# Gate panels moved in between index scores and attention heads, kept in device memory until the projections

## The reference, cut to what matters

```
(fq, fk, fv, ff, dq, dk, dv, iq, ik, iw, mq, g) = jnp.split(u @ w_in[l], SPLIT_POINTS, axis=-1)
o_a = fox_attention(fq, fk, fv, logf)                       # 8 heads of 64, causal with a forget bias
o_b = dsa_attention(dq, dk, dv, iq, ik, iw, k_sel)          # 8 heads of 64 on the 128 best keys by index score
o_c = memory_attention(mq, km, vm)                          # 4 heads of 128 on 256 memory rows
branches = jnp.stack([o_a, o_b, o_c], axis=2)
proj = jnp.einsum('bsnw,nwd->bsnd', branches, w_branch[l])  # 512 -> 1024 for each branch
gates = jax.nn.sigmoid(g.reshape(B, S, N_BRANCHES, D))
h = h + jnp.sum(gates * proj, axis=2) @ w_out[l]
```

## Time and profile before

| | us |
|---|---|
| runs | 2604.82, 2604.82, 2608.97 (median 2604.82) |
| the profiled execution | 2603.45 |
| its span, first to last instruction | 2601.7 |
| PE busy | 2461.6 (95%) |
| DVE busy | 1348.6 (52%) |
| ACT busy | 875.1 (34%) |
| POOL busy | 120.6 (5%) |
| mean granted clock of PE | 0.959 of full |

### The profile page before, as it was taken

One profiled execution on the slowest core, in us unless ns is written; L12 is line 12 of the kernel. 1 busy time (PEld: TensorE's weight loads), 2 busy tenths in 40 slices (PEclk: granted clock), 3 DMA queues, 4 the chain that ended last, 5 costly groups with the idle time before them and its releaser, 6 DMA issues.

```text
span 2601.7 us, 32023 instructions
## 1 busy us (share of the span) xinstructions
PE 2461.6 (95%) x12976; PEld 1952.7 (75%) x12976; DVE 1348.6 (52%) x2043; ACT 875.1 (34%) x1461; POOL 120.6 (5%) x156
## 2 busy tenths in 40 slices
PE   7999999997989999999999998888898899999997
PEld 6888888874444888888888886777776687788886
DVE  5444344426683546544433673443375663777723
ACT  4222223321455223322222344334346243433321
POOL 0000000000233000000000000132200000000000
PEclk9999999897699999999999997899898999999998
DMA  5333333320000333333333331000031132233331
GB/s 164 97 97 93 102 102 109 90 69 1 1 1 1 96 90 109 98 97 97 97 95 97 92 83 49 2 2 2 2 90 41 49 97 81 73 97 97 99 95 49
DMA packets 366419, 189.04 MB, mean 73 GB/s; under 512 B 11328, under 2 KB 363840, under 8 KB 366272
## 3 DMA queue, kind: packets, MB, share of 16 engines
q1 hardware_dynamic: 366272, 187.00, 25.2%
HBM read 184.87 MB, written 2.10 MB: 72 GB/s over the span
## 4 chain that ended last, share of the span: by engine, by line
PE 88%; DVE 7%; ACT 3%; issue 1%; DMA 0%; POOL 0%; DVEq 0%; SPq 0%; ACTq 0%
PE ps L429 22%; PE ps L431 22%; PE ps L430 22%; PE ps L677 2%; PE ps L948 1%; PE ps L696 1%; PE ps L915 1%; PE ps L1879 1%; PE ps L1881 1%; PE ps L1880 1%; PE ps L811 1%; PE ps L1373 1%; PE ps L1368 1%; PE ps L541 1%; PE ps L1363 1%
## 5 line engine op out<-in xcount | busy, mean ns | idle before, releaser
L429 PE MATMUL ps<-u_hi,w_hi 128*128 128x512 f32 (+1 forms) x1800 | 706.4, 392 | 3.0 <-DVE w_lo L362 2.1
L430 PE MATMUL ps<-u_lo,w_hi 128*128 128x512 f32 (+1 forms) x1800 | 703.9, 391 | 0.0
L431 PE MATMUL ps<-u_hi,w_lo 128*128 128x512 f32 (+1 forms) x1800 | 703.7, 391 | 0.0
L362 DVE TENSOR_TENSOR w_lo<-w_raw,w_hi 128x1024 fp32r<-128x1024 f32 (+2 forms) x366 | 422.6, 1155 | 271.8 <-ACT w_hi L378 270.9
L378 ACT ACTIVATE w_hi<-w_raw 128x1024 fp32r<-128x1024 f32 (+2 forms) x366 | 365.7, 1000 | 445.7 <-PE ps L431 417.1
L429 PEld LDWEIGHTS ps<-u_hi,w_hi 128*128 128x128 f32 (+1 forms) x1800 | 336.0, 187 | 79.7 <-DVE w_lo L362 3.0
L430 PEld LDWEIGHTS ps<-u_lo,w_hi 128*128 128x128 f32 (+1 forms) x1800 | 336.0, 187 | 75.2 <-issue 1.6
L431 PEld LDWEIGHTS ps<-u_hi,w_lo 128*128 128x128 f32 (+1 forms) x1800 | 336.0, 187 | 74.7 <-issue 0.8
L431 PE MATMUL ps<-mid_hi,w_lo 128*128 128x512 f32 x528 | 208.7, 395 | 0.0
L429 PE MATMUL ps<-mid_hi,w_hi 128*128 128x512 f32 x528 | 208.7, 395 | 0.0
L430 PE MATMUL ps<-mid_lo,w_hi 128*128 128x512 f32 x528 | 208.7, 395 | 0.0
(11 more groups left out here) (397 smaller groups left out, 3178.3 us busy)
## 6 DMA issues: line engine op xcount, KB each, us to landing
w_raw<-w_in_dram SPq DMA_DIRECT2D x101, 512.0 KB, 3.8
w_raw<-ffn_w_gate_dram SPq DMA_DIRECT2D x44, 512.0 KB, 3.9
w_raw<-ffn_w_up_dram SPq DMA_DIRECT2D x44, 512.0 KB, 3.9
w_raw<-w_up_dram SPq DMA_DIRECT2D x44, 512.0 KB, 3.8
w_raw<-ffn_w_down_dram SPq DMA_DIRECT2D x32, 512.0 KB, 3.7
w_raw<-w_out_dram SPq DMA_DIRECT2D x24, 512.0 KB, 3.6
w_raw<-w_down_dram SPq DMA_DIRECT2D x16, 512.0 KB, 3.6
w_raw<-ffn_w_down_dram SPq DMA_DIRECT2D x16, 384.0 KB, 3.2
```

The lines of the kernel that those rows point to most:

```text
L362: dve.tensor_tensor(lo, raw, hi.bitcast(F32), ALU.subtract).then_inc(w_split, 1)
L429: pe.matmul(out, wh, h_k, start=k0 + k == 0, stop=False)
L430: pe.matmul(out, wh, l_k, start=False, stop=False)
L431: mm = pe.matmul(out, wl, h_k, start=False, stop=end)
```

## The change

The 24 gate panels become a segment of their own, `gates`, ahead of the branches. A generator on PE, `gate_panels_pe`, holds their k blocks, and `feed` issues the next one or two of them: after every index product one, after every fourth two (40 k blocks, 5 panels), and two at four spots of each job until they are used up (152 k blocks in the jobs 0 to 18). The last job gets none. The gates use the banks 3 and 2; to free bank 3, the single transposed block of key block 3 now goes into the unused first quarters of bank 2, and ACT copies both at once.

DVE scales a finished gate panel (`gate_keep_dve`). The first three stay in `gate_first`. The other 21 go by way of `part` and `acc` to a tensor in device memory, `gate_rows`, 256 KB each (`store_gate`), and come back into `gate_back`, a ring of 16 places that lies where `u_hi` and `u_lo` were (`load_gate`). Six loads are issued at once when all gate panels are used and stored, the rest one behind each weight panel. ACT makes the sigmoid in place, one panel ahead of its use. The upper and lower parts of the weight panels that follow are made within the index steps and the jobs.

The branches then hold 8 projection panels each. In the last one the upper part of the sum moves from DVE to ACT (`mix_upper_act`), and DVE makes the lower part one panel later (`mix_lower_dve`).

```diff
-        def source(i, j, n=n, wb=wb):
-            if j % 2 == 0:
-                return w_in[:, :, bass.ds(i * (2 * P) + (O_G + n * D + j // 2 * P), P)]
-            return wb[:, :, bass.ds(i * (2 * P) + j // 2 * P, P)]
-        seg(f"branch{n}", 4, 4, source, [8, 4, 8, 4], P, [0, 1, 2, 3])
+        seg(f"branch{n}", 4, 2, lambda i, j, wb=wb: wb[:, :, bass.ds(i * (4 * P) + j * P, P)], [4] * 4, P, [0, 1, 2, 3])
     columns("out1", kblocks(T["w_out"][0]), 0, 4, 2)
     gate_up("ffn2_up", kblocks(T["ffn2_w_gate"][0]), kblocks(T["ffn2_w_up"][0]), 0)
     down("ffn2_down", kblocks(T["ffn2_w_down"][0]))
@@ -311,7 +307,92 @@
     idx_mm, idx_relu, idx_acc, idx_sel = sem("idx_mm"), sem("idx_relu"), sem("idx_acc"), sem("idx_sel")
     sc_inv = sem("at_inverse")
     sc_mm, sc_max, sc_exp, sc_norm, pt_mm, pt_out, pv_mm, pv_out = (sem("at_" + n) for n in ("scores", "max", "exp", "norm", "transposed", "copied", "product", "out"))
-    o_ready, mix_ready, mix_split, gate_on = sem("o_ready"), sem("mix_ready"), sem("mix_split"), sem("gate_on")
...
+    GATES, KEPT, GATE_RING = 3 * DK, 3, 16
+    gate_rows = nc.dram_tensor("gate_rows", (GATES, P, SEQ), F32).ap()
+    gate_first, _ = fixed("gate_first", [P, KEPT, SEQ], F32, ZONE + 30 * SEQ * 4)
...
+    def store_gate(sp, m):
+        sp.wait_ge(bank_read, segs["gates"].group + m + 1 + BANKS)
+        sp.dma_start(gate_rows[m], gate_stage(m)).then_inc(gate_stored[m % 2], 16)
+    def load_gate(sp, m):
+        if m == KEPT:
+            sp.wait_ge(w_used, segs["gates"].base + GATES + RING)
+            for i in range(2):
+                sp.wait_ge(gate_stored[i], 16 * len([x for x in range(KEPT, GATES) if x % 2 == i]))
+        if m >= KEPT + GATE_RING:
+            sp.wait_ge(bank_read, segs["branch0"].group + m - GATE_RING + 1 + BANKS)
+        sp.dma_start(gate_tile(m), gate_rows[m]).then_inc(gate_in[(m - KEPT) % GATE_RING], 16)
+    GATES_AT_ONCE = 6
...
+    def load_weights_and_gates(sp):
+        base = segs["gates"].base
+        after = segs["branch0"].base + 7
+        for n in range(base, after + GATES - KEPT - GATES_AT_ONCE):
+            m = n - base - 8
+            if KEPT <= m < GATES:
+                store_gate(sp, m)
+            if n == after:
+                for x in range(KEPT, KEPT + GATES_AT_ONCE):
+                    load_gate(sp, x)
+            load_weights(sp, n, n + 1)
+            if n >= after:
+                load_gate(sp, KEPT + GATES_AT_ONCE + n - after)
+        return after + GATES - KEPT - GATES_AT_ONCE
+    def gate_panels_pe(pe):
+        s = segs["gates"]
+        for m in range(GATES):
+            n = s.base + m
+            pe.wait_ge(w_split, n + 1 + RING)
+            pe.wait_ge(bank_read, s.group + BANKS + (m - 1 if 1 <= m < 5 else m))
+            out = gate_bank(m)
+            for k in range(DK):
+                wh, wl = w_hi[:, n % RING, k, :], w_lo[:, n % RING, k, :]
+                pe.matmul(out, wh, u_hi[:, k, :], start=k == 0, stop=False)
+                pe.matmul(out, wh, u_lo[:, k, :], start=False, stop=False)
+                mm = pe.matmul(out, wl, u_hi[:, k, :], start=False, stop=k == DK - 1)
+                if k == DK - 1:
+                    mm.then_inc(w_used, 1)
+                yield
+    def feed(panels, blocks):
+        for _ in range(blocks):
+            next(panels, None)
+    def gate_keep_dve(dve, m):
+        s = segs["gates"]
+        out = gate_tile(m)
+        if m >= KEPT:
+            out = gate_stage(m)
+            if m >= KEPT + 2:
+                dve.wait_ge(gate_stored[m % 2], 16 * ((m - KEPT) // 2))
+        dve.wait_ge(w_used, s.base + m + 1 + RING)
+        dve.tensor_tensor(out, gate_bank(m), rms[:, :], ALU.mult).then_inc(bank_read, 1)
...
-    def index_pe(pe):
+    def index_pe(pe, panels):
...
+                feed(panels, 2 if n % 4 == 3 else 1)
                 n += 1
+    INDEX_UPPER, INDEX_KEEP = (2, 8, 14, 21, 27), (7, 13, 20, 26)
...
+                if n in INDEX_UPPER:
+                    gate_upper(act, INDEX_UPPER.index(n))
...
+                if n in INDEX_KEEP:
+                    gate_keep_dve(dve, INDEX_KEEP.index(n))
+                if n in INDEX_UPPER:
+                    gate_lower(dve, INDEX_UPPER.index(n))
...
-        return [t for t in DOWN if t < len(jobs[n].v)]
+        return (2, 1, 0) if jobs[n].kind != "mem" else (1, 0)
...
-                    pe.wait_ge(pt_out, turn_count(n - 1, t) if t < len(jobs[n - 1].v) else turned(n - 2) if n > 1 else 0)
+                    pe.wait_ge(pt_out, turn_count(n - 1, t) if t in turns_of(n - 1) else turned(n - 2))
...
+                    if t == 2 and q == 3:
+                        pe.transpose(ps[2][:, P:2 * P], probs[:, n % 2, 3, 3 * P:4 * P], ident)
...
         for n in range(NJ):
             scores(n, (3, 2))
+            feed(panels, 2)
             if n:
                 turn(n - 1, (1, 0))
+            feed(panels, 2)
             scores(n, (1, 0))
+            feed(panels, 2)
             if n:
                 product(n - 1)
-            turn(n, (3, 2))
+            feed(panels, 2)
+            turn(n, (2,))
...
+                first = P if t == 2 else j.first[t]
+                act.activation(keysT[:, t, first:SEQ], ps[t][:, first:SEQ], ACT.Copy).then_inc(pt_out, 1)
...
+            if n + 5 < GATES:
+                gate_upper(act, n + 5)
...
+                if q == 3:
+                    gate_keep_dve(dve, n + 4)
...
+                if q == 2 and n + 5 < GATES:
+                    gate_lower(dve, n + 5)
...
+    def gate_sigmoid_act(act, m):
+        if m < KEPT:
+            act.wait_ge(bank_read, segs["gates"].group + m + 1 + BANKS)
+        else:
+            act.wait_ge(gate_in[(m - KEPT) % GATE_RING], 16 * ((m - KEPT) // GATE_RING + 1))
+        act.activation(gate_tile(m), gate_tile(m), ACT.Sigmoid).then_inc(gate_on, 1)
...
     def branch_act(act, n):
+        if n == 0:
+            gate_sigmoid_act(act, 0)
         for i, g in sums(act, f"branch{n}"):
-            for j, _, read, _ in g:
+            for j, _, _, _ in g:
+                m = i * len(g) + j
                 upper_parts(act, f"branch{n}", i, j)
-                if j % 2 == 0:
-                    gate = pair_a[:, j // 2, :]
-                    act.wait_ge(bank_read, read)
-                    act.activation(gate, gate, ACT.Sigmoid).then_inc(gate_on, 1)
+                if DK * n + m + 1 < GATES:
+                    gate_sigmoid_act(act, DK * n + m + 1)
+                if n == 2 and m:
+                    mix_upper_act(act, m - 1)
+        if n == 2:
+            mix_upper_act(act, DK - 1)
...
+    def mix_lower_dve(dve, k):
+        dve.wait_ge(mix_upper, k + 1)
+        dve.tensor_tensor(mix_lo[:, k, :], mix[:, k, :], mix_hi[:, k, :].bitcast(F32), ALU.subtract).then_inc(mix_split, 1)
...
+            for b in (0, 1):
+                branch_split(dve, st, 1, b)
         for i, g in sums(dve, name):
-            for m in range(2):
-                (_, used_g, _, bank_g), (_, used_p, read_p, bank_p) = g[2 * m:2 * m + 2]
...
+            for j, used, read, bank in g:
+                m = i * len(g) + j
+                dve.wait_ge(gate_on, DK * n + m + 1)
+                dve.wait_ge(w_used, used)
                 if n == 0:
-                    dve.tensor_tensor(mm, bank_p[:, :], pair_a[:, m, :], ALU.mult).then_inc(bank_read, 1)
-                    if i < 2:
-                        for b in (0, 1):
-                            branch_split(dve, st, 1 + i, 2 * m + b)
+                    dve.tensor_tensor(mix[:, m, :], bank[:, :], gate_tile(m), ALU.mult).then_inc(bank_read, 1)
                 else:
-                    dve.tensor_tensor(part[:, :], bank_p[:, :], pair_a[:, m, :], ALU.mult).then_inc(bank_read, 1)
-                    dve.wait_ge(bank_read, read_p)
-                    st.done(dve.tensor_tensor(mm, mm, part[:, :], ALU.add))
-                if n == 2:
-                    split_dve(dve, st, mm, mix_hi[:, 2 * i + m, :], mix_lo[:, 2 * i + m, :], mix_split)
-                lower_behind(dve, name, i, 2 * m + 1)
+                    gated = (part, acc)[m % 2][:, :]
+                    dve.tensor_tensor(gated, bank[:, :], gate_tile(DK * n + m), ALU.mult).then_inc(bank_read, 1)
+                    dve.wait_ge(bank_read, read)
+                    x = dve.tensor_tensor(mix[:, m, :], mix[:, m, :], gated, ALU.add)
+                    if n == 2:
+                        x.then_inc(mix_added, 1)
+                    else:
+                        st.done(x)
+                lower_behind(dve, name, i, j)
+                if n == 0 and m < 6:
+                    branch_split(dve, st, 1 + (m + 2) // 4, (m + 2) % 4)
+                if n == 2 and m:
+                    mix_lower_dve(dve, m - 1)
+        if n == 2:
+            mix_lower_dve(dve, DK - 1)
...
-            load_weights(sp, segs["fox_qkv"].base + RING, N_PANELS)
+            load_weights(sp, segs["fox_qkv"].base + RING, segs["gates"].base)
```

(32 more changed lines are left out.)

27 lines of the change are left out of this document (14 added, 13 removed).

## The result

The changed kernel takes 2587.16 us (median of 4 runs, 2586.98 to 2588.27) against 2605.89 for the kernel before in the same runs (2604.82 to 2608.97): a ratio of 0.9927, with an interval of 0.991 to 0.9944. The forecast was 2582. The profiled execution took 2587.11, its span is 2585.3. PE is busy for 2462.0 us, as long as before, in a span that is 16.4 us shorter: what went, on balance, is idle time.

A forecast was written before the change was run, and what follows sets the result against it. PE bounds the kernel: full in the branches, but with waits and half clock ahead of them. Room -31.6, switching +5.6, clock +3 and branches +1 give -22.0, from 2603.45 to 2581.4, said as 2582; range 2567 to 2599.

The forecast's parts named there:

- room of 31.6 us: From first index product to branches, 202.1 us: the part that is not PE's own work at full clock, 31.6 us.
- Changes (a): Index stage and jobs: PE going from part-array product to full-array k block costs 0.11 us at 51 spots, 5.6 lost.
- end of 2567: Best end: 0.21 us weight loads of 32 index products hide behind k blocks, switching costs nothing; gain 36, time 2567.
- The clock (b): Start of the index stage: half speed for some 5 us loses 2.5, taken as 3.
- thinnest cover: Mem jobs: DVE needs 9.5 us against PE's 10.8, a margin of 1.3 us; its work was costed at nothing.
- wait of 1 us that was put: Last branch: DVE needs 3.3 us per panel against PE's 2.73, so about 1 us shows in `out1`.
- the end that is worked out is 2597: Slow end: switching at all 108 spots, clock 10 us late, waits left; 24.9 lost of 31.6, time 2597.
- Half clock through the index scores: Rival: the filled index stage stays at half clock, 51 us more than in the sum, 2632; chance 0.07.
- the pairs that the prediction priced at 9.8: Index products overlapping on different array halves: kept paired they take 13.9 us instead of 23.7, making the result 9.8 lower.
- The waits stay: Rival: all 21.3 us of PE waits ahead of the branches remain beside the k blocks, 2603; chance 0.09.
- Projections late: Rival in the branches: DVE or late gates set 3.3 us for each of 24 panels, 13.7 more, 2595; chance 0.09.
- More gain: Rival: index stage and jobs gain more, through hidden weight loads and free switching, 2571; chance 0.13.

## Why the prediction was right, point by point

- **The room of 31.6 us was filled but for 2.5 of waits, and 22.0 of it kept.** From the first index product to `out1` the forecast was 400.1-22.0 = 378.1, and the trace has 378.1. The exactness is luck in part: the index stage came out 4.3 above its share, the jobs 3.2 below and the branches 1.1 below.
- **Changes (a), mis-sized in the index stage.** The sum took 0.11, from the only place where the earlier trace rows showed one. Entering a single index product costs as much as leaving it: 691.14-690.81 = 0.33, and 692.52-692.19 = 0.33, each 0.10 above the usual 0.23. With 0.21 for 32 steps that is 6.7 where 3.5 was put. The end of 2567 counted on the 0.21 of a score that stands for no columns, which the prediction took for a weight load in the open, to go behind a k block. It didn't: a single product of 512 columns costs 1.05 there too. So that end was out of reach with the pairs parted.
- **The clock (b).** 0.50 lasted 9.0 us, from 637.9 to 646.9: 4.5 lost where 3 was put. 23.7+27.2+6.7+4.5 = 62.1 then gives the stage's 61.7. How long 0.50 lasts is partly luck: the same instructions had it for 3.4 us in the execution with 24 added products, and the stage was 2.6 shorter.
- **The jobs.** Five fox jobs take 13.38 each (forecast 13.36), without a wait. A dsa job takes 13.10 (13.19) and a mem job 10.5 to 10.9 (10.95), and the way from the mem jobs to the dsa jobs 12.40 in one step. That makes some 2 of the 3.2; the rest is not itemised. The thinnest cover, DVE in a mem job, held but for two waits of 0.43:

```profile
825.47 0.47 PE L370 MATMUL ps<-u_hi,w_hi 128*128 128x512 f32 x1 [0.43 <-DVE part L389]
```

- **The branches.** From 948.71 to 1016.00 PE is full, 67.3 (forecast 67). DVE takes from 1005.07 to 1007.87 for a panel, 2.80, as PE does, yet `out1` starts without the wait of 1 us that was put:

```profile
1015.77 0.39 PE L512 MATMUL ps<-o_hi,w_lo 128*128 128x512 f32 x1
1016.00 0.40 PE L510 MATMUL ps<-mix_hi,w_hi 128*128 128x512 f32 x1
```

  The loads came in time: no sigmoid held PE up, at a DMA share of 0.51.
- **What failed: everything behind `out1` was taken as unchanged.** It cost 5.1 us in the profiled execution, and with the start 0.6 later that is the whole of the 5 us between 2582 and 2587.16. The sum had no term for a stretch that the change doesn't touch.
- **The range.** Its upper bound of 2599 follows from no sum: the end that is worked out is 2597. The result is far from either.
- **The rivals.** *Half clock through the index scores* did not come: 0.50 past 650 was its sign, and 646.9 ended it. The experiments show that it was close at hand in another sense: the index stage gave nothing at all, and the jobs all, and the pairs that the prediction priced at 9.8 were worth 11.8 and 3.4 of changes with them. *The waits stay* fell: 15.5 us of them went with the jobs' blocks alone. *Projections late* fell with PE full. *More gain* was there to be had, but not in this placing: with pairs kept the change is worth 36 us, not 19.

## What to carry to other kernels

Before independent work is put between small products, look whether those overlap in pairs: put it behind the pair, since a filler that parts them can eat all that it fills. Filler can pay twice where it stands in waits, once for the wait and once for a clock that doesn't fall; so the best places are the earliest ones, ahead of the stage that suffers from the slow clock. And spread it over as many spots as the dependent work has pieces: longer runs at fewer spots saved changes and brought the waits back.

## What the runs showed of the hardware that was not expected

- Two float32 products with 64 rows on different halves of the array, issued one behind the other, cost 1.06 us for 512 columns at 2.4 GHz, and one alone 1.05.
- A float32 product with 64 rows between products on all of the array costs 0.10 us on entering and 0.10 on leaving at 2.4 GHz (0.33 from start to start in place of 0.23).
- At one place of the program PE waits for the search's result. Behind a wait of 2.11 us it had 1.2 GHz up to about 816, behind one of 1.80 it fell for 3.4 us, behind one of 0.9 in a full stream it kept 2.4 GHz, and so it did behind one of 2.19 in the kernel before. The length of the wait alone doesn't decide.
- The same instructions of the index stage had 1.2 GHz for 9.0 us in one execution and for 3.4 in another.
- A stretch of 3648 small products, the same in every kernel, took between 398.9 and 404.4 us. In the changed kernel and the kernel before PE's busy time there is 354.3 and 349.6, the granted clock 0.91 and 0.93; DVE and ACT are as busy in both.
